# State-space block of a one-core Trainium2 kernel: all projections ahead of the groups, y kept feature-major, no GpSimd work in it

## What is computed

```python
proj = h @ w_in                       # 1024 -> z 2048 | x 2048 | B,C fwd and bwd, 4 x 1024 | dt 64
xbc = silu(centred_depthwise_conv(xbc, conv_w, conv_b))      # 5 taps over the tokens
dt = softplus(dt_raw + dt_bias); a = -exp(a_log)             # 2 directions x 32 heads
cum = cumsum(dt * a)                                         # in chunks of 128 tokens
scores = (C @ B.T) * exp(where(lower, cum_q - cum_k, -inf))  # 8 groups of B/C, 4 heads each
y = scores @ (x * dt) + (C @ carried_state) * exp(cum)       # forward; the same, flipped, backward
y = rmsnorm((y_fwd + y_bwd + x * d_skip) * silu(z), norm_g)
h = h + y @ w_out                                            # 2048 -> 1024
```

## Time and profile before

| | |
|---|---|
| runs | 1847.86 us median of 3 (1847.75 to 1848.11) |
| the profiled execution | 1844.54 us, span of the core 1842.7 us |
| mean granted TensorE clock | 0.965 |
| TensorE matmuls, weight loads | 1764.4 us busy, 1498.4 us busy |
| VectorE, ScalarE, GpSimd | 1103.0, 871.0, 261.9 us busy |
| HBM read | 297.97 MB, 162 GB/s over the span |

### The profile page before, as it was taken

How to read it: one execution, slowest core, us unless ns; L and a number is a source line. 1 busy time by engine, 2 the same in 40 slices (tenths; PEclk the granted TensorE clock), 3 DMA queues, 4 the chain that set the end, 5 groups by cost and what they waited for, 6 DMA issues and landing times.

```text
span 1842.7 us, 22946 instructions
## 1 busy us (share of the span) xinstructions
PE 1764.4 (96%) x9270; PEld 1498.4 (81%) x9270; DVE 1103.0 (60%) x1415; ACT 871.0 (47%) x1195; POOL 261.9 (14%) x159
## 2 busy tenths in 40 slices
PE   6999999888879999999999999999999999999998
PEld 5888789877867888888888857888889988888886
DVE  4554448888974655475545685654565456476543
ACT  5444446444334544374445565544463354545532
POOL 0000001565650000000000430000000134200000
PEclk9999999877779999999999989999999999999999
DMA  8555565543334655558655513755555522356552
GB/s 272 183 183 174 169 190 156 142 110 97 115 115 142 204 187 177 188 180 241 200 171 194 178 39 106 225 183 193 172 191 176 160 92 92 114 173 203 175 178 83
DMA packets 239992, 300.57 MB, mean 163 GB/s; under 512 B 9360, under 2 KB 167440, under 8 KB 239888
## 3 DMA queue, kind: packets, MB, share of 16 engines
q1 hardware_dynamic: 234512, 289.78, 49.6%
q10 hardware_dynamic: 5376, 9.33, 2.1%
HBM read 297.97 MB, written 1.11 MB: 162 GB/s over the span
## 4 chain that ended last, share of the span: by engine, by line
PE 85%; DVE 9%; DMA 4%; ACT 1%; issue 1%; SPq 0%; DVEq 0%; POOL 0%; ACTq 0%
PE bank L489 81%; PE bank L492 4%; DMA E<-cum 3%; DVE E L1898 3%; DVE Wt L1680 3%; DVE cv L1683 1%; ACT whi L1188 1%; DVE wlo L1680 0%; DMA h<-in_x 0%; DVE cbm L1680 0%; DMA pT<-in_pT 0%; ACT th L1185 0%; DVE bc L1683 0%; ACT hThi L1188 0%; ACT xn L1185 0%
## 5 line engine op out<-in xcount | busy, mean ns | idle before, releaser
L1680 DVE TENSOR_TENSOR wlo<-raw,whi 128x2048 fp32r<-128x2048 f32 (+2 forms) x254 | 552.2, 2180 | 357.8 <-ACT whi L1188 357.7
L1188 ACT ACTIVATE whi<-raw 128x2048 fp32r<-128x2048 f32 (+2 forms) x284 | 518.1, 1831 | 290.6 <-PE bank L489 288.9
L489 PE MATMUL bank<-whi,hThi 128*128 128x512 f32 x1136 | 450.7, 397 | 2.5 <-DVE wlo L1680 2.5
L489 PE MATMUL bank<-wlo,hThi 128*128 128x512 f32 x1136 | 443.2, 390 | 0.3 <-DVE wlo L1680 0.2
L489 PE MATMUL bank<-whi,hTlo 128*128 128x512 f32 x1136 | 428.3, 391 | 0.7 <-DVE hTlo L1683 0.7
L489 PEld LDWEIGHTS bank<-whi,hThi 128*128 128x128 f32 x1136 | 214.0, 188 | 47.7 <-ACT whi L1188 2.9
L489 PEld LDWEIGHTS bank<-whi,hTlo 128*128 128x128 f32 x1136 | 213.6, 188 | 47.0 <-DVE hTlo L1683 1.6
L489 PEld LDWEIGHTS bank<-wlo,hThi 128*128 128x128 f32 x1136 | 213.9, 188 | 43.4 <-DVE wlo L1680 1.1
L489 PE MATMUL bank<-hThi,whi 128*128 128x256 f32 (+2 forms) x784 | 230.7, 294 | 0.0
L489 PE MATMUL bank<-hTlo,whi 128*128 128x256 f32 (+2 forms) x784 | 225.8, 288 | 0.0
L489 PE MATMUL bank<-hThi,wlo 128*128 128x256 f32 (+2 forms) x784 | 225.4, 287 | 0.0
(11 more groups left out here) (203 smaller groups left out, 2177.1 us busy)
## 6 DMA issues: line engine op xcount, KB each, us to landing
raw<-in_ffn_w_gu SPq DMA_DIRECT2D x172, 512.0 KB, 4.9
raw<-in_ffn_w_down SPq DMA_DIRECT2D x40, 1024.0 KB, 5.1
raw<-in_w_in SPq DMA_DIRECT2D x30, 1024.0 KB, 5.2
raw<-in_ssd_w_in SPq DMA_DIRECT2D x16, 1024.0 KB, 5.4
raw<-in_ssd_w_in SPq DMA_DIRECT2D x32, 512.0 KB, 5.5
raw<-in_w_up SPq DMA_DIRECT2D x16, 1024.0 KB, 5.4
raw<-in_w_down SPq DMA_DIRECT2D x16, 1024.0 KB, 5.0
raw<-in_na_w_qkv SPq DMA_DIRECT2D x12, 1024.0 KB, 5.3
```

What stands on the lines that cost most here:

```text
L489: return T.e.matmul(out, lhsT, rhs, start=start, stop=stop, skip_group_check=skip)
L1188: return e.activation(out, in_, ACT.Identity, **kw)
L1680: return e.tensor_tensor(out, a, b, op)
```

## The change

The block is rebuilt; nothing outside it changes, except that SyncE's loads of `pT` and of a row now wait for y(6) and y(7).

- Order of the tiles: dt first, then for each of the eight groups z, x, B/C forward, B/C backward (the list `SSD_TILES`, 32 tiles), then the eight `yout` tiles. All 32 are projected feature-major with 48 matmuls of 256 columns, in banks 0 to 3 in turn. z is feature-major too, so the gate is applied feature-major.
- All convolved tiles stay in SBUF (`xTs`, `bc`) and get a full SiLU of ScalarE. `pool_tiles` leaves out the block's tiles, so VectorE splits all of them.
- The step size is put into the exponent: `lnd` is ln(dt) (dt is first raised to at least 1e-30), `cml` is the sum minus `lnd`, `bo` the sum to the end of the chunk plus `lnd`. One operation of VectorE subtracts `cml` and caps at `lnd`, sixteen of them for a group; eight activations of ScalarE (128x128, with `bo` as bias) make the block across the chunks. So `xd`, `xdd` and all of GpSimd's work but the last root fall away.
- The weights are stored as two blocks of 256 columns and two of 128 for each head (`weights`) in two buffers, EW0 and EW1; EW1 lies where `hThi` and `hTlo` were. VectorE multiplies them by C*B with six operations for a group (two masked halves from `cbm`, the blocks across from PSUM).
- y is feature-major: x (128 tokens by 64) is stationary, the weights are the moving side, four matmuls (256, 128, 128, 256 columns, fp32) for each head. No transposes of y. The skip is added by VectorE from PSUM, the gate by VectorE.
- The sum of squares goes through TensorE (`squares`: ScalarE squares into `gate`, matmuls with a 2-wide pattern) and VectorE (`ssr`), and is turned at the end.
- The groups are written one ahead on every engine; the `yout` tile of the group before stands in the loop of each group.

More of the change, by code:

```diff
@@ L749, in ssd @@
             norm()
[L750 to L760, removed]
             hi, lo = take("dt")
@@ L772, in project_x, with project @@
+            def project(i):
+                label, b = SSD_TILES[i], i % 4
+                hi, lo = take(*label)
                 clear(b)
                 featmajor(bank_half(b, 0), hi, lo, 0, hThi, hTlo)
[L774 to L781, removed]
@@ L794, in ssd @@
[L794 to L800, removed]
+                if i == 0:
+                    dt_rows()
+                featmajor(bank_half(b, 1), hi, lo, P, hThi, hTlo).then_inc(*sig(*named(label)))
@@ new lines, in project, with products @@
+                empties[b] = ("gate", label[1]) if label[0] == "z" else ("conv",) + label + (4, 1)
+            def products(g):
+                clear(4, 5)
+                for d in range(2):
+                    B, C = bcs[:, g, 2 * d, :], bcs[:, g, 2 * d + 1, :]
[6 more added lines that the diff above has]
+                empties[5] = ("wmul", g, 2, 1)
@@ L1453, in ssd @@
+            for i, label in enumerate(SSD_TILES):
+                if i:
+                    take(*label)
+                    silu(i - 1)
+                taps(i)
+                if i == 1:
+                    column_sums()
+                    fetch(0)
+            silu(31)
+            e.preload_act_table_set("natural_log_exp_and_others")
             decays(0)
+            x_rows(0)
             for g in range(8):
                 if g < 7:
-                    tanh(g + 1, 0)
-                products(g)
@@ L1475, in ssd @@
[L1475 to L1477 removed]
+                    fetch(g + 1)
+                    decays(g + 1)
+                    x_rows(g + 1)
+                columns_of(g)
+                if g == 7:
                     ple_load(0)
@@ L1840, in ssd @@
             norm()
-            for c in range(4):
-                for k in range(2):
-                    take("z", c, k)
             take("dt")
-            take("x", 0)
+            take("z", 0)
             V.wait_ge(*at("dtm"))
@@ L1939, in ssd @@
+            for i, label in enumerate(SSD_TILES):
+                if i:
+                    take(*label)
+                if i == 2:
+                    column_sums()
+                conv(i)
             decays(0)
+            products(0)
             for g in range(8):
                 if g < 7:
-                    project(g + 1, 0)
-                products(g)
-                if g < 7:
-                    take("bc", g + 1, 1)
+                    decays(g + 1)
+                    products(g + 1)
+                outputs(g)
```

589 lines of the change are left out of this document (209 added, 380 removed).

## The result

The changed kernel takes 1869.09 us, the median of four executions (1866.83 to 1869.35), where the kernel before takes 1847.88. The ratio is 1.0112, with a 95% interval of 1.0094 to 1.0129: 21 us slower. I had forecast 3 us slower, 1851, in a range of 1834 to 1869. The direction and the chain came out as forecast; the size did not, and the time stands at the upper edge of the range.

What follows compares the result with a forecast made beforehand. Before: groups bound by VectorE plus a fetch, projections by TensorE. After: projections to 405.4, second fetch at 415.1, 23.1 us periods, tail to 593.1 against 590.58; +3 in all, from 1847.9 to 1851 us, range 1834 to 1869.

Steps and rivals of the forecast that it cites:

- bank-5 wait: TensorE's squares of group g-1 wait for VectorE's third product of group g+1, idling TensorE some 6 us and delaying the output tile.
- the fetch issued ahead of ScalarE's pending work: ScalarE's queue issues the next decay-row fetch without waiting for pending copies, only for what its queue has waited on.
- rival (a): In the groups, weight tile yout g-1 is released early: period 17.9 us, kernel about 1820 us; chance 0.06.
- join, to the second fetch's issue: Between projections and groups: taps, convolution, SiLU, table load and first exponentials, 9.7 us until ScalarE issues the second fetch.
- to the third product, five: VectorE in each group, from fetch landing through sixteen subtractions, two masks and three products: 5.8 us, over five periods.
- tail: After group 7's landing: last outputs, squares, output tiles and splits until the next stage's first matmul, 36.8 us.
- One fetch (L): The 1 MB fetch of decay rows for each group lands 7.8 us after issue, with ends 5.4 and 9.5.
- The subtraction: VectorE's sixteen subtractions at each group's start take 3.15 us without GpSimd's split beside them.
- The burst: TensorE's squares and 24 output-tile matmuls per group, starting at low clock: 9.4 us, ends 6.5 and 12.3.
- Rival (c): In the groups, TensorE's clock stays low through burst (12.3 us) and fp32 work: period 26 to 27, about 1868; chance 0.18.
- Rival (d): Projections lose their cover because VectorE's work or loads come late: +12 us, about 1863; chance 0.06.
- Rival (b): In the groups, the fetch lands in 6.0 us or the burst runs all fast; either alone about 1838; chance 0.2.

## Why the prediction was right in direction and wrong in size

**What bounds it, and the join of waits: right.** The bank-5 wait, the release of yout g-1, the fetch behind the split, and the fetch issued ahead of ScalarE's pending work all stand in the chain. Undoing the first gave 5.8 us a group, so it did hold the chain; rival (a) fell.

**The account.** By the next stage's first matmul, at 615.41 us in the profile after, I was 22.3 us short of it (593.1). The landings of the loop are at 427.7, 448.7, then 474.6 to 578.9 in five periods; forecast 422.9, 440.8 and 23.1 us a period.

| term | forecast | measured | share of the 22.3 |
|---|---|---|---|
| start of the block | as in the trace of before | 2.8 us later | +2.8 |
| projections | left at 405.4 | 409.86, 1.7 of its own | +1.7 |
| join, to the second fetch's issue | 9.7 | 9.57 | -0.1 |
| landing of group 1 | 7.8 | 8.28 | +0.5 |
| landing of group 2 | 7.8 | 10.91 | +3.1 |
| landings, five periods | 7.8 | 10.37 mean | +12.8 |
| to the third product, five | 5.8 | 6.8 | +5.0 |
| squares and output tile, five | 9.4 | 8.74 mean | -3.3 |
| tail | 36.8 | 36.5 | -0.3 |

The 22.3 us are those of the two profiles. The sum had 3.8 us on top for hops and for the way to the median, and the rest of the kernel took 0.5 us less, so 18 us remain between 1851 and the median measured.

**The step that failed is "One fetch (L)".** I took 7.8 us, below the least of the eight rows, on the argument that the late landings were those beside weight loads and that the one load left would come behind. It costs 16.4 of the 22.3 us. The argument misread the trace of before. All eight fetches ran beside 0.85 to 1.12 MB of weights, the three that took 7.9 to 8.1 us too; this is the queue of the weights and the landing, first from 378 us, then from 521 us:

```profile
q1 hardware_dynamic: 1878, 0.95, 34.2%
...
E<-cum ACTq DMA_DIRECT2D x1, 1024.0 KB, 9.5
```

```profile
q1 hardware_dynamic: 246, 0.94, 26.0%
...
E<-cum ACTq DMA_DIRECT2D x1, 1024.0 KB, 7.9
```

The bytes beside the two are the same. Their packets were small, some 0.5 KB, beside the five fetches that took 8.6 us or more and large, some 4 KB, beside the three others. So these rows never showed that a fetch with less beside it is quicker. The load is issued some 4 us after each fetch and slows it, but by 1.4 us only. The rest was not a matter of that neighbour: alone, the fetches of the loop take 8.0 to 9.4. Why the same fetch landed in 7.9 to 8.1 beside 0.94 to 1.00 MB of weights in the last three groups of the kernel before, and takes 9.0 to 9.4 alone in most groups here, no run shows. I had set the fetch beside a weight tile of the same 1 MB at 5.4 and looked at bytes alone; the difference was in the row all along, and the thing to ask was what differs between the two transfers, which is the rows that they share and the size of their pieces.

The Trainium skill (DMA: Bandwidth & Descriptors, Bandwidth) has 6.15 us for 1 MB, measured on a transfer that GpSimd issues and as the time that the DMA engines are busy. This chip took 10.2 for shared pieces of 2 KB, 5.2 for the same pieces unshared and 4.7 for shared pieces of 8 KB, from issue to landing. The measurements decide: one figure by size does not price this transfer, and the prediction left out that the figure was for another issuer and another span of time.

**The subtraction** was sized by the rows of the kernel before, with one scalar pointer. The row was right for that form: with the immediate sixteen take 3.22 against 3.15 forecast. The new form has two, and I did not see that it is another operation: +1.0 a group.

**The burst** was right to 7% and the clock as said, low for the squares and the first matmuls, full after. It rose 4.6 us after the squares had begun (granted 0.50 to 485.6 us, 1.00 from 486.1), where I had 6.1, and that makes most of the difference. TensorE idled 12.4 us ahead of it, not 6: its fp32 work of a group ran at the full clock behind the burst, eight, four and 32 matmuls in 5.5 us from 490.07, where I had 7.2, and the longer landing did the rest. Neither the idle time nor the fp32 work was on the path. Rival (c) named 1868 us, and that number came out by accident: its mechanism, a burst at 12.3 us, did not occur.

**The projections** kept their cover, as said: TensorE is busy 197.6 of the 198.4 us from 211.5, at 0.98 of its clock. Rival (d) fell. Rival (b) fell for this kernel; for the layout in 8 KB pieces it is the case, and its 1838 us stands near the 1833.75 measured, though its sum, with 4.7 us put in for its 6.0, would give about 1829.

**The start of the block.** It moves by itself: TensorE's first transposes of the norm stand at 209.1 to 212.1 us in these profiles, 208.66 in that of before, and the runs that do not differ up to there spread as widely as that. The profile after, 211.48, is one of the late ones, so the 2.8 us in the table are not shown to be an effect of the change.

**VectorE's gain** from the missing GpSimd work was real, and the account had to show where it went. TensorE, VectorE and the fetch each have under 14 us of work for a group; the change strung them into one loop of 26. Three moves in the order of the program take 77 us off.

## What to carry to other kernels

When each engine's work for a group is well under the period, write out the loop of releases and look for a program order that makes an urgent step stand behind one that is not: here a shared bank between unrelated matmuls, and a fetch behind a split. Cut one link and the next loop shows, so go on until one engine has no wait left; it is the bound, and another that is nearly as busy may only be waiting for it. Where a chain shows an engine idle for no named reason, look in the program for the semaphore that it waits on. And when two transfers of one size differ in the trace, compare their pieces and addresses before their neighbours: laying the rows out in one piece was worth as much as a reordering.

## What I had not expected of the hardware

- 1 MB to 128 partitions as 512 pieces of 2 KB from the same four rows lands in 9.8 us, from 512 rows in 5.2, as 8 KB pieces that all partitions share in 4.7.
- Such a fetch slows what runs beside it: the weight loads issued from 400 to 590 us landed after 7.2 us in the median in the changed kernel, up to 9.1, and after 4.8, up to 5.7, with the 8 KB pieces.
- VectorE's 128x128 subtraction with cap takes 283 ns with one pointer scalar and an immediate, 340 to 348 ns with two pointers.
- GpSimd's split of 4.5 us added 3.8 to 4.3 us to VectorE's sixteen subtractions beside it; one of them, 0.34 us long, took 4.52.
